# The last key-tail transpose and its copy, moved behind the next scores in an attention pipeline

## The reference

```python
# differential, layer 0
s = einsum('bqhcd,bshcd->bhcqs', qb, k) * scale + bias
p = softmax(s, axis=-1)
out = einsum('bhqs,bshv->bqhv', p[:, :, 0] - lam * p[:, :, 1], v)
# plain, layer 0
out = einsum('bkgqs,bskd->bqkgd', softmax(einsum('bqkgd,bskd->bkgqs', qb, k) * scale), v)
# window, layer 1: 16 meta keys and a band of 384
s = where(visible, einsum('bqkgd,bskd->bkgqs', qb, kc) * scale + bias, NEG_INF)
p = softmax(concatenate([s, sink_col], -1), -1)[..., :-1]
out = einsum('bkgqs,bskd->bqkgd', p, vc)
```

## Time and profile before

| | |
|---|---|
| three runs | 3982.75, 3988.9, 3989.41 us (median 3988.9) |
| profiled execution | 3982.75 us, span 3981.0 us |
| TensorE, VectorE, ScalarE, GpSimd busy | 94%, 47%, 30%, 4% of the span |
| mean granted TensorE clock | 0.959 of full |
| attA in the trace | about 147 to 305 us |
| attC in the trace | about 816 to 915 us |

### The profile page before, as it was taken

How to read it: one execution, slowest core, us unless ns; L and a number is a source line. 1 busy time by engine, 2 the same in 40 slices (tenths; PEclk the granted TensorE clock), 3 DMA queues, 4 the chain that set the end, 5 groups by cost and what they waited for, 6 DMA issues and landing times. The chain is left out here.

```text
span 3981.0 us, 50543 instructions
## 1 busy us (share of the span) xinstructions
PE 3729.4 (94%) x20367; PEld 3086.3 (78%) x20367; DVE 1852.8 (47%) x2483; ACT 1193.4 (30%) x1741; POOL 165.7 (4%) x202
## 2 busy tenths in 40 slices
PE   8899999899999799999999899979899999989997
PEld 8759999867888576777888688858677788868885
DVE  6465334355433334366554533342526655454333
ACT  3353222254222342232232322224423223322222
POOL 0000000000000000002310000000000132000000
PEclk9899999999999899998999899989999899999998
DMA  3102222112222212220012122211122000212222
GB/s 122 52 1 86 96 85 96 68 42 76 105 95 85 79 43 83 76 74 22 1 38 95 64 95 100 89 66 64 53 95 74 32 1 17 95 64 102 93 92 82
DMA packets 48937, 278.88 MB, mean 70 GB/s; under 512 B 10134, under 2 KB 12694, under 8 KB 19419
## 3 DMA queue, kind: packets, MB, share of 16 engines
q1 hardware_dynamic: 48700, 275.88, 19.8%
q10 hardware_dynamic: 30, 0.13, 0.0%
HBM read 273.73 MB, written 2.22 MB: 69 GB/s over the span
## 5 line engine op out<-in xcount | busy, mean ns | idle before, releaser
L317 PE MATMUL ps<-xs,ffn_w 128*128 128x512 f32 x2112 | 483.5, 391 | 29.4 <-DVE xs L633 29.4
L317 PEld LDWEIGHTS ps<-xs,ffn_w 128*128 128x128 f32 x2112 | 399.3, 189 | 114.1 <-issue 31.0
L317 PE MATMUL ps<-u,mlp_w 128*128 128x264 f32 (+1 forms) x2880 | 455.5, 321 | 9.7 <-DVE u L633 9.7
L317 PEld LDWEIGHTS ps<-u,mlp_w 128*128 128x128 f32 x2880 | 416.6, 189 | 48.3 <-issue 10.5
L317 PE MATMUL ps<-hn,mlp_w 128*128 128x264 f32 (+1 forms) x2304 | 363.7, 320 | 0.0
L317 PEld LDWEIGHTS ps<-hn,mlp_w 128*128 128x128 f32 x2304 | 332.4, 188 | 30.4 <-issue 0.5
L317 PE MATMUL ps<-xs,cv_w 128*128 128x512 f32 x1152 | 278.5, 402 | 8.4 <-DVE cv_w L627 8.4
L317 PEld LDWEIGHTS ps<-xs,cv_w 128*128 128x128 f32 x1152 | 218.5, 191 | 75.2 <-issue 23.0
L317 PE MATMUL ps<-ff,ffn_w 128*128 128x512 f32 x1056 | 240.0, 389 | 0.0
L411 ACT CAST ffn_w<-raw 128x2048 fp32r<-128x2048 f32 (+1 forms) x74 | 124.1, 1676 | 373.7 <-PE ps L317 333.7
L317 PEld LDWEIGHTS ps<-ff,ffn_w 128*128 128x128 f32 x1056 | 198.3, 188 | 41.1
(11 more groups left out here) (402 smaller groups left out, 5058.2 us busy)
## 6 DMA issues: line engine op xcount, KB each, us to landing
raw<-in_w_ffn_up SPq DMA_DIRECT2D x44, 1024.0 KB, 4.8
raw<-in_w_up SPq DMA_DIRECT2D x32, 1024.0 KB, 4.8
raw<-in_w_down SPq DMA_DIRECT2D x32, 1024.0 KB, 4.8
raw<-in_w_conv SPq DMA_DIRECT2D x24, 1024.0 KB, 4.8
raw<-in_w_ffn_down SPq DMA_DIRECT2D x32, 704.0 KB, 4.1
raw<-in_w_mqk SPq DMA_DIRECT2D x10, 1024.0 KB, 4.9
raw<-in_w_qk_even SPq DMA_DIRECT2D x9, 1024.0 KB, 4.9
raw<-in_w_mv SPq DMA_DIRECT2D x8, 1024.0 KB, 4.8
```

Source lines behind the costliest of these rows:

```text
L317: ins = nc.tensor.matmul(bank(u)[:, h, :], w[:, s, wp, k * g.bw + j * P:k * g.bw + (j + 1) * P], g.xs[:, xp, k, h * n:(h + 1) * n], start= ...
```

## The change

In each job, `turn_meta(i, 3)` moves on TensorE from before `score(n+3)` to the end of the step (`turn_meta(i, 2)` stays ahead of it), and `copy_meta(i)` moves on VectorE from before `top(n+3)` to behind it, and behind `invert(i)` where there is one. Nothing is added or removed, and no wait is changed.

```diff
@@ TensorE, step n
-                        for uu in ((), (), (0, 1), (2, 3))[u]:
+                        for uu in ((), (), (0, 1), (2,))[u]:
                             turn_meta(i, uu)
                     if n + LEAD < NS:
                         score(n + LEAD)
@@
                     if i >= 1 and u < 3:
                         values(i - 1, u)
+                    if 0 <= n < NS and u == NU - 1:
+                        turn_meta(i, u)
@@ VectorE, step n
-                    if 0 <= n < NS and u == NU - 1:
-                        copy_meta(i)
                     if n + LEAD < NS:
                         top(n + LEAD)
                     if n in (1 - LEAD, 2 - LEAD) and not window:
                         top_queries(2 * (n - 1 + LEAD))
-                    if 0 <= n < NS and u == NU - 1 and not diff[i]:
-                        invert(i)
+                    if 0 <= n < NS and u == NU - 1:
+                        if not diff[i]:
+                            invert(i)
+                        copy_meta(i)
```

## The result

The changed kernel takes 4006.82 us (median of five, 4004.05 to 4012.59) against 3987.77 (3981.07 to 3989.41): ratio 1.0054, 95% interval 1.0039 to 1.0068. The profiled execution took 4006.8 us, 24.0 us of span more than the one of before.

The account below looks back on a forecast made before the run. It took TensorE to bound attC and a TensorE-VectorE loop attA's differential jobs. Terms 7.5 + 0.65 + 2.15 - 1.2 - 0.35 = +8.75 us put the median at 3997.6; forecast 3997, range 3988 to 4006.

Parts of the forecast that it names:

- The late copy in attC: attC, jobs 1 to 6: the first value matmul waits 1.25 us a job for the moved copy, +7.5 us.
- the clock falls: Rival, attC: new gaps lower TensorE's clock; 9 us for one job (4006.6), 54 us for all six (4051); chance 0.07.
- attA, job 0: Meta queries at the head of `turn_queries` wait for the copy and start 2.15 us late; nothing takes that back: +2.15 us.
- 2 us either way: attA: the 2.15 us delay may lengthen or shorten the neighbouring stretch at low clock, by 2 us either way.
- attA, jobs 1 and 2: Differential jobs: without the copy ahead of `top`, the maxima come 0.60 us earlier a job, -1.2 us for two.
- job 3: attA, counted with jobs 3 to 6: `top` waits for scores, so 0.05 to 0.1 us gained each, -0.35 for four.
- attC, jobs 0 and 7: First and last job of attC: copy and its reader 0.35 and 0.3 us later, together +0.65 us.
- The slot of a copy on VectorE: attA's differential jobs: the copy takes 0.60 us of VectorE; the skill's drain would make the slot 1.07 us.
- the rival of a VectorE that bounds: Rival, attA and attC: late maxima everywhere, so the move pays 0.60 us in 14 jobs, -8.4 us (3980.5); chance 0.03.

Follow-up runs that it names:

- fill_c: Changed kernel plus one 128x512 matmul a job in attC, ahead of the wait for the copy, its result overwritten: 3992.9 us, ratio 1.0019 to before.
- half_fill_c: Changed kernel plus a half-length 128x256 matmul a job in attC, ahead of the wait for the copy: 3990.9 us, ratio 1.0016 to before.

## Why the prediction was wrong

- **The late copy in attC: right, and its wait nearly so.** Forecast 1.25 us a job, released by the copy, ahead of the value matmul; measured 1.08 of idle and 1.12 of spacing. Most of the difference is the wake, 0.25 after a copy of 0.63, where I took 0.30 and 0.67. As a term, 6.7 us instead of 7.5.
- **The step that failed is the clock in attC: the sum has no term for it, and the rival "the clock falls" was priced too coarsely and given 0.07.** I argued from attA's differential jobs: TensorE busy 0.90 of the time at clock 1.00, as it would be in attC. The runs show that this doesn't carry over. attC at 0.91 busy (11.28 of 12.35) loses the clock in four or five of the six spacings in all four profiles of the changed attC with its gap of 1.1 us, in five or none with 0.8, and in none with 0.25 or none. What differs between the two stages beside the gap (the loop's work, the length of the matmuls) wasn't taken apart. The price of a job with a fall was 9 us in my text; it is 1.6 us (13.97 for 12.35) in most, and 4.7 (17.1) in the worst, since the clock is reduced for a part of the job. What the sum put at nothing was 6.6 us between copies 1 and 6 in the first profile and 16.0 in the second. The range ended at the price of one whole job at the low clock, 4006.6, and the time, 4006.8, came of several partial falls; that the two numbers are so near is chance.
- The Trainium skill, "TensorE: Matmul & The Clock Gate", section "A second HAM failure mode: psum-queue depth-cycling", has short idles between matmul groups swing the clock between its levels. The trace agrees: granted clock 0.78 to 0.90 in the stretch from copy 1 to copy 6, and 1.00 once the idle is filled.
- **attA, job 0: the late start was right, the claim that nothing takes it back was not.** Forecast a start 2.15 us late; against the negation of step 6, the turned queries started 1.13 us ahead of it before (173.23 to 174.36) and 0.81 us behind it after (173.76 to 172.95): 1.94 us later. But from attA's first `top` to the first value matmul of job 1 the five profiles with attA as before take 59.2 to 61.3 us (mean 60.6), and four of the six changed ones take 60.8 to 61.1 (mean 60.9), from which the 0.58 us gained behind job 1's copy is already gone. By these means the late start costs some 0.9 us there and not 2.15, and the spread of the five, 2.1 us, is as wide as the forecast term, so the size stays rough. In the other two changed profiles that stretch is 65.3 and 66.7 us. What follows comes and goes: attA as changed took 153.1, 153.2, 153.2, 153.9, 157.6 and 159.0 us, as before 152.9 to 155.0. In one of the two long ones, the changed kernel's first profile, TensorE stays at the lower level, 1.2 of 2.4 GHz, almost all the way from `turn(4)` to the end of the scores of step 8 (mean 0.51), where before the mean was 0.66. The stretch in the trace after, and then in the one before:

```profile
178.49:203.10 24.61, 23.60 (x117) 18.34 (x117) 4.37 (x12) 5.37 (x19) 0.39 (x2) 0.51 0.06 20
```

```profile
177.41:197.47 20.06, 19.05 (x117) 14.82 (x118) 4.28 (x12) 5.35 (x19) 0.40 (x2) 0.66 0.07 24
```

- I gave this 2 us either way; that stretch is 4.6 longer. That the late start brings it about is not shown: two of six profiles against none of five would come about by chance in some one case of four (an estimate: of the 55 ways to place two long ones among eleven, 15 have both among the six).
- **attA, jobs 1 and 2: right; job 3: missed.** The waits behind the copies of jobs 1 and 2 are 0.60 us for 1.18, and copies 1 and 2 are 13.64 apart for 14.23. I counted job 3 among those whose `top` waits for the scores and gave it 0.05 to 0.1 us; its wait falls from 0.63 to 0.17, a gain of 0.46. Copies 2 and 3 don't show this, 13.60 apart for 13.10, since the copy itself moves; the first value matmuls of jobs 2 and 3 do, 13.60 for 14.06. The plain jobs 4 to 6: value matmuls 15.20 apart for 15.3, the 0.1 us of the transpose.
- **attC, jobs 0 and 7.** Forecast 0.65 together. At job 7 the matmul waits 1.38 us for 1.15, at job 0 it waits 0.21 in the first profile of the changed kernel and not at all in the second: 0.2 to 0.5.
- **The slot of a copy on VectorE.** The 0.60 us was borne out by what jobs 1 and 2 gained. The section of the Trainium skill that the prediction quotes on it, "VectorE: DVE Perf Modes", section "The DRAIN you can't avoid", also says that a next operation that isn't held starts earlier; the prediction leaves this out, and the row need not speak against the section.
- **VectorE's cover in attC, the rival of a VectorE that bounds: as argued.** VectorE's work is 38.6 us in the stretch in every kernel, and its place in line costs nothing but the copy's.
- Together: the waits in attC are 6.7 us and 0.2 to 0.5 in jobs 0 and 7. In attA the forecast was +0.6; four changed profiles have a mean of 153.3 us and the five of before 154.2, and the other two are 157.6 and 159.0. The waits are about 7 us, and most of what is left of the 19 to 21 is the clock in attC: between copies 1 and 6 it is 6.6 us in the first profile of the changed kernel and 77.54 - 56.17 - 5.4 = 16.0 in the second. The kernels `fill_c` and `half_fill_c`, which take the falls of the clock out and leave the late copy, are 1.0019 and 1.0016, that is 7.6 and 6.4 us over before, near the sum of 8.75 that had no clock in it.

## What to carry to other kernels

A consumer's slack is measured from the end of its input to its own start, here 1.34 us, and a move that costs more than that is paid on the full engine, however idle the moving engine is. When a change puts a gap into a stretch of TensorE that had none, price the matmuls around it at the lower clock too: here that was 6.6 us in one profile and 16.0 in another, for gaps of 5.4 us in both. A filler matmul tells the price of the gap and that of the clock apart in one run. A neighbouring stage that keeps its clock with gaps of the same size is no proof that this one will.

## What the runs showed of the hardware

- A gap of 0.8 us in every 12.1 us of an otherwise full TensorE went both ways: one profile at clock 1.00 over the whole stretch, one, on another chip, at 0.87, the same kernel and the same waits, 7.8 us apart.
- Useless matmuls made the changed kernel faster: 1.0019 and 1.0016 with a filler, 1.0054 and 1.0051 without.
- TensorE's first matmul after a wait for VectorE's copy starts 0.25 us after the copy's end when the engine has stood 1.08 us, and 0.05 us after when it has stood 0.25.
